# Reordering ScalarE's queue in the attentions of a two-block transformer kernel: a unit's high half ahead of the exponentials, the copy of turned probabilities ahead of the filling unit's evacuation

## The chip, the core and the metric

One core of a Trainium2 chip runs the whole program. The metric is device time in microseconds of one execution; the kernel before has a median of 2870.46 us over three runs.

## What is computed

Two blocks of two layers each, on one sequence of S = 256 tokens with D = 1024 channels, all in float32. A layer of the first block mixes tokens in three ways (8-head forgetting attention with a causal mask, a short convolution, a chunkwise gated recurrence), projects back, and then applies a SwiGLU (layer 0) or a routed mixture of eight experts (layer 1). A layer of the second block runs three attentions side by side, all with 8 heads:

```python
y_a = _gqa_axial(q, k, v, ...)          # softmax(q k) v, rotary by row and column
y_b = _diff_attention(q, k, v, lam, ..) # (softmax(q1 k1) - lam * softmax(q2 k2)) v
y_c = _mla(c_q, c_kv, k_r, ...)         # latent attention
merged = jnp.sum(gates * jnp.einsum('bsne,ned->bsnd', y, w_branch[l]), axis=2)
x = x + merged @ w_out[l]
x = x + jnp.square(jax.nn.relu(h2 @ w_ff1[l])) @ w_ff2[l]
```

## The kernel before

**Weights come as units.** All weight matrices are cut into 550 units of 128 x 2048 float32 (1 MB). Each engine has its own program, and all take the units in the same order. SP loads unit s into `raw[s % 4]` (L451) once VectorE has finished with the unit four before it. TensorE's fast path takes numbers in two parts, so ScalarE copies the unit to its high half, `whi[s % 3]` (`split_hi`, L500), after the load has landed and after TensorE has used unit s - 3, and VectorE then subtracts it from the unit to get the low half, `wlo[s % 3]` (`split_lo`, L843). TensorE multiplies in three products (high by high, high by low, low by high, `mm3`), all recorded at L1373. ScalarE and VectorE split two units ahead of the one that TensorE works on: `take()` on each of them moves the stream on by one unit and splits unit s + 2 (LEAD = 2). Except for the loads' queue, nothing is scheduled at run time: the order of each engine is that of its program, and semaphores tie them together.

**Projections.** `out_of(bank, dst, ...)` on ScalarE (L524) is: `take()`, wait until TensorE has used the unit, then evacuate the PSUM bank into its place in SBUF (L527).

**Attentions.** An attention is a list of jobs, each of four heads and 128 queries. Before it, projections that are not yet needed are put into a list of *fillers* on every engine; the attention takes one of them in every iteration, or in every second one (`fill_every=2`), so that TensorE has something to do while ScalarE and VectorE work on a softmax. A filler's product always goes to PSUM bank 7, and TensorE starts the next filler only when bank 7 has been evacuated. The loop has two iterations more than there are jobs. In iteration n:

- TensorE (`attention`, L1472): scores of job n into banks 0 and 1 or 2 and 3; then, for job n - 2, the weighing of the values with the turned probabilities `pt`, into bank 6 (it waits for the copy of `pt`); then the filler, 48 matmuls of 256 columns into bank 7; then the transposes of job n - 1's probabilities (L1519, `ident`) into banks 4 and 5, once VectorE has normalized them.
- VectorE (L917): in the first mixer, bias and mask (L932) and row maximum (L936), else the row maximum straight from PSUM (L938); then, if there is a filler, the low half of a unit (L843), and behind the first mixer's first filler also the short convolution (L976 to L983), which waits for that filler's evacuation; then it waits for the exponentials, takes the reciprocal of the sums (L944), and normalizes (L946). In the difference attention every second job is combined with the one before it (L950), and only these jobs are transposed and weighed.
- ScalarE (L549): four exponentials (L563, each with its sum), after the maximum; the evacuation of bank 6 for job n - 2 (`y` or `yT`, L568); then the filler (`fill`, L529, in iterations that have one): the high half of the unit two ahead (L500) and the evacuation of bank 7 (L527); then the copy of the transposed probabilities of job n - 1 from banks 4 and 5 to `pt` (L579), once TensorE has turned them.

There are eight attentions in the program: in each of two layers of the first block one `fox_heads` attention of 4 jobs (6 iterations, 2 fillers: `cc1`, and `rgs` with the function Silu); in each of two layers of the second block an axial one of 4 jobs (6 iterations, 6 fillers), a difference one of 8 jobs (10 iterations, `fill_every=2`, 5 fillers: Tanh into `sg`), and a latent one of 4 jobs without fillers. ScalarE's functions come from tables; a change from Exp to Silu or back puts a table load ahead of the instruction, while the copies run under any table, and Exp and Tanh without a load between them.

The order inside ScalarE's iteration is what the change touches:

Of the kernel before, what the change touches and what calls it, by code (L numbers as in the profile page):

```python
# [114 lines left out]
def build(nc, io):  # L115
    ctx = ExitStack()
    with ctx:
        def sem(name):
            return ctx.enter_context(nc.semaphore(name))
# [4 lines left out]
        hi_ready, lo_ready, unit_used = sem("hi_ready"), sem("lo_ready"), sem("unit_used")  # L124
# [3 lines left out]
        drained = sem("projection_drained")  # L128
# [95 lines left out]
        PS = ctx.enter_context(nc.psum_tensor("PS", [P, 8, 512], F32))  # L224

        def banks(b, n):
            return PS[:, b:b + n, :].rearrange("p b c -> p (b c)")
# [255 lines left out]
        def scalar_program(act):  # L483
            C = Counts()
            stream = Count()
            fillers = []

            def after(sem, k=1):
                act.wait_ge(sem, C.next(sem, k))
# [6 lines left out]
            def split_hi(s):  # L496
                act.wait_ge(raw_landed[s % RAW], 16 * (s // RAW + 1))
                if s >= SPLIT:
                    act.wait_ge(unit_used, s - SPLIT + 1)
                act.activation(whi[s % SPLIT][:], raw[s % RAW][:], ACT.Copy).then_inc(hi_ready, 1)  # L500

            def take():

                s = stream.next() - 1
                if s + LEAD < U_ALL:
                    split_hi(s + LEAD)
                return s + 1
# [16 lines left out]
            def out_of(bank, dst, scale=1.0, func=ACT.Copy, wide=None):  # L524
                act.wait_ge(unit_used, take())
                src = PS[:, bank, :] if wide is None else PS[:, bank, :].rearrange("p (t c) -> p t c", t=wide)
                act.activation(dst, src, func, scale=scale).then_inc(drained, 1)  # L527
                C.next(drained)

            def fill(n=1):  # L530
                for _ in range(min(n, len(fillers))):
                    f = fillers.pop(0)
                    out_of(7, f.dst, f.scale, f.func, f.wide)

            def head_square(src, sq):
                act.activation(sq, src, ACT.Square).then_inc(hn_squared, 1)

# [5 lines left out]
            def head_norm(src, nt, rows_, scale, sq):  # L543
                head_square(src, sq)
                fill()
                head_root(SUMS, rows_, scale)
                fill()

            def attention(jobs, pbs, pts, fill_every=1):  # L549
                turned_before, mixed_before = C.now(turned), C.now(mixed)  # L550
                turns = list(itertools.accumulate(j.value is not None for j in jobs))
                k = 0
                for n in range(len(jobs) + 2):
                    if n < len(jobs):
                        j, pb, b, w = jobs[n], pbs[n % PB], 2 * (n % 2), jobs[n].keys
                        sp = PS[:, b:b + 2, :].rearrange("p b (h k) -> p b h k", h=2)
                        m, z = stat[:, n % PB, 0:4], stat[:, n % PB, 4:8]
                        if n >= PB:
                            act.wait_ge(turned, turned_before + turns[n - PB + (jobs[n - PB].value is None)])
                        after(max_ready)  # L560
                        for i in range(4):
                            src = pb[:, i, 0:w] if j.bias else sp[:, i // 2, i % 2, 0:w]
                            ins = act.activation(pb[:, i, 0:w], src, ACT.Exp, bias=m[:, i:i + 1],  # L563
                                                 accum_out=z[:, i:i + 1])
                        ins.then_inc(exped, 1)
                    if n >= 2 and jobs[n - 2].value:
                        after(mixed)
                        act.activation(jobs[n - 2].dst, PS[:, 6, 0:2 * P].rearrange("p (t q) -> p t q", t=2),  # L568
                                       ACT.Copy).then_inc(mixed_out, 1)
                        C.next(mixed_out)  # L570
                    if n % fill_every == 0:
                        fill()
                    if 1 <= n <= len(jobs) and jobs[n - 1].value:
                        kb = jobs[n - 1].keys // P
                        tp = banks(4, 2).rearrange("p (h b q) -> p h b q", h=4, b=NT)
                        after(turned)
                        if k >= 2:
                            act.wait_ge(mixed, mixed_before + k - 1)
                        act.activation(pts[k % 2][:, :, 0:kb, :], tp[:, :, 0:kb, :], ACT.Copy).then_inc(pt_ready, 1)  # L579
                        k += 1  # L580

            def first_mixer(l):
                out_of(6, flat(zf))
# [26 lines left out]
                out_of(6, pair(qkT, 3))  # L610
                act.wait_ge(drained, C.now(drained))
                head_square(qkT[:], hT[:])
                cum_exp()
                out_of(7, vtok[:, :, 0:UC], wide=NT)
# [9 lines left out]

                fillers.extend(waiting_projections1(l))
                attention(fox_heads(l), pb1, pt1)
                fill(len(fillers))

# [88 lines left out]
            def second_mixer(l):  # L717
# [11 lines left out]
                after(va_turned)  # L729
                act.activation(va[:].rearrange("p t c -> p (t c)"), PS[:, 4, 0:S], ACT.Copy).then_inc(va_ready, 1)  # L730
                attention(axial_heads(), pb2, pt2)

                fill(max(0, len(fillers) - 15))
                fill()
                fill()
                C.next(rope_done)
                attention(diff_heads(), pb2, pt2, fill_every=2)
                act.wait_ge(mixed_out, C.now(mixed_out))
                head_norm(y2[:, 4:8, :], 4, 16, 1.0 / HD, hT[:, 0:4, :])
# [1227 lines left out]
        with nc.Block() as block:  # L1967
            block.sync(sync_program)
            block.scalar(scalar_program)
            block.vector(vector_program)  # L1970
            block.tensor(tensor_program)
# [160 lines left out]
```

## Time and profile before

| | |
|---|---|
| runs | 2867.01, 2870.46, 2870.82 us |
| profiled execution | 2872.48 us, its span 2870.7 us |
| TensorE matmul busy | 2617.0 us, 91% |
| VectorE busy | 1857.6 us, 65% |
| ScalarE busy | 1496.9 us, 52% |
| TensorE's granted clock, mean | 0.948 |
| copies to `pt`, L579 | 32, 31.2 us |
| exponentials, L563 | 160 |
| high halves, L500 | 550 of 1.91 us, 1051.9 us |
| low halves, L843 | 550 of 2.29 us, 1259.5 us |

The times of matmuls overlap: one of 256 columns is recorded with about 0.28 us, and the next starts about 0.12 us behind it. "Idle before" of a row is the time for which its engine did nothing, with the instruction that ended the wait. The clock is told as a share of 2.4 GHz, and has two levels, 1.0 and 0.5. A row of the timeline with x4 or x16 stands for so many instructions, its duration from the first's start to the last's end.

### The profile page before, as it was taken

Reading aid. Unit: us, or ns where it says so; the run is one execution under the profiler, and the core shown is the slowest. Engines: PE = TensorE matmul, PEld = TensorE weight load, DVE = VectorE, ACT = ScalarE, POOL = GpSimd, SP = SyncE. Lnnn points to the kernel's source line nnn. Section 1 sums busy time; section 2 is a strip of 40 time slices with the busy share of each in tenths; the row PEclk is TensorE's granted clock in tenths of the full one; section 3 lists DMA queues with packets and bytes.
Section 4 is the critical chain, followed back from the end, with each engine's and each line's share of the span. In section 5 each row is a group of like instructions: output and inputs, shape, how many; then the busy total and the mean of one; then the engine's idle time right before and its main releaser. Section 6 shows DMA issues by size and latency. Waiting matters only on the chain.

```text
span 2870.7 us, 38623 instructions
## 1 busy us (share of the span) xinstructions
PE 2617.0 (91%) x16826; PEld 2329.6 (81%) x16826; DVE 1857.6 (65%) x1580; ACT 1496.9 (52%) x1442; POOL 0.2 (0%) x4
## 2 busy tenths in 40 slices
PE   6879999887899999999999997988799989878998
PEld 6769998766787878878787786877689988768998
DVE  4645445564688888888888885555565554546554
ACT  4244334433577777777776774445444444544443
POOL 0000000000000000000000000000000000000000
PEclk9879999997999999999999998999899999889999
DMA  5214554221499989989999894323145543223452
GB/s 203 89 59 146 178 190 149 101 89 59 177 366 349 368 348 360 355 347 367 348 364 351 352 358 169 133 89 133 44 162 180 189 145 118 83 94 116 149 191 89
DMA packets 83100, 585.32 MB, mean 204 GB/s; under 512 B 9481, under 2 KB 11209, under 8 KB 12273
## 3 DMA queue, kind: packets, MB, share of 16 engines
q1 hardware_dynamic: 82928, 582.81, 54.4%
q8 instruction: 135, 2.21, 0.3%
q14 instruction: 37, 0.30, 0.0%
HBM read 581.73 MB, written 1.05 MB: 203 GB/s over the span
## 4 chain that ended last, share of the span: by engine, by line
PE 82%; DVE 10%; ACT 6%; issue 1%; DMA 0%; ACTq 0%; SPq 0%; DVEq 0%
PE PS L1373 80%; ACT whi L500 2%; DVE wlo L843 2%; ACT pb L563 2%; PE PS L1757 1%; PE PS L1519 1%; ACT pt L579 1%; DVE hT L860 1%; DVE stat L938 1%; DVE pb L946 1%; DVE small L856 1%; DVE hT L911 0%; DVE pb L932 0%; DVE qe L1004 0%; DVE ke L1003 0%
## 5 line engine op out<-in xcount | busy, mean ns | idle before, releaser
L843 DVE TENSOR_TENSOR wlo<-raw,whi 128x2048 fp32r<-128x2048 f32 x550 | 1259.5, 2291 | 568.3 <-ACT whi L500 558.3
L500 ACT ACTIVATE whi<-raw 128x2048 fp32r<-128x2048 f32 x550 | 1051.9, 1913 | 375.5 <-PE PS L1373 374.6
L1373 PE MATMUL PS<-hhi,whi 128*128 128x256 f32 x1952 | 572.3, 293 | 31.9 <-DVE hlo L866 19.0
L1373 PE MATMUL PS<-hlo,whi 128*128 128x256 f32 x1952 | 563.3, 289 | 0.0
L1373 PE MATMUL PS<-hhi,wlo 128*128 128x256 f32 x1952 | 562.5, 288 | 0.0
L1373 PEld LDWEIGHTS PS<-hhi,whi 128*128 128x128 f32 x1952 | 384.9, 197 | 46.7 <-issue 40.4
L1373 PEld LDWEIGHTS PS<-hlo,whi 128*128 128x128 f32 x1952 | 385.9, 198 | 0.6 <-issue 0.5
L1373 PEld LDWEIGHTS PS<-hhi,wlo 128*128 128x128 f32 x1952 | 385.1, 197 | 0.0
L1373 PE MATMUL PS<-whi,xghi 128*128 128x512 f32 x896 | 360.1, 402 | 2.1 <-ACT pm L667 2.1
L1373 PE MATMUL PS<-whi,xglo 128*128 128x512 f32 x896 | 355.2, 396 | 0.0
L1373 PE MATMUL PS<-wlo,xghi 128*128 128x512 f32 x896 | 355.0, 396 | 0.0
L1373 PEld LDWEIGHTS PS<-whi,xglo 128*128 128x128 f32 x896 | 169.2, 189 | 40.7
L1373 PEld LDWEIGHTS PS<-whi,xghi 128*128 128x128 f32 x896 | 169.2, 189 | 40.6 <-issue 2.1
L1373 PEld LDWEIGHTS PS<-wlo,xghi 128*128 128x128 f32 x896 | 169.3, 189 | 37.5
L1373 PE MATMUL PS<-whi,mahi 128*128 128x512 f32 x448 | 177.9, 397 | 1.9 <-DVE malo L1191 1.9
L1373 PE MATMUL PS<-whi,malo 128*128 128x512 f32 x448 | 178.0, 397 | 0.0
L1373 PE MATMUL PS<-wlo,mahi 128*128 128x512 f32 x448 | 177.9, 397 | 0.0
L1373 PE MATMUL PS<-bhi,wlo 128*128 128x256 f32 x512 | 144.1, 281 | 0.0
L1373 PE MATMUL PS<-bhi,whi 128*128 128x256 f32 x512 | 143.7, 281 | 0.0
L1373 PE MATMUL PS<-blo,whi 128*128 128x256 f32 x512 | 142.6, 279 | 0.0
L563 ACT ACTIVATE pb<-PS,stat 128x256 f32<-128x256 f32 x128 | 58.9, 472 | 116.6 <-DVE stat L938 109.3
L1373 PEld LDWEIGHTS PS<-whi,mahi 128*128 128x128 f32 x448 | 84.8, 189 | 22.1 <-DVE wlo L843 2.1
(331 smaller groups left out, 3720.2 us busy)
## 6 DMA issues: line engine op xcount, KB each, us to landing
raw<-in_wm SPq DMA_DIRECT2D x336, 1024.0 KB, 4.9
raw<-in_ws SPq DMA_DIRECT2D x214, 1024.0 KB, 4.8
xT<-in_xT SPq DMA_DIRECT2D x1, 1024.0 KB, 4.8
bsum<-in_bsum SPq DMA_DIRECT2D x1, 1024.0 KB
out_T<-hT SPq DMA_DIRECT2D x4, 256.0 KB, 2.5
lmask<-in_lmask SPq DMA_DIRECT2D x1, 512.0 KB
tri<-in_tri SPq DMA_DIRECT2D x1, 256.0 KB
cmask<-in_cmask SPq DMA_DIRECT2D x1, 256.0 KB
```

Source lines behind the costliest of these rows:

```text
L500: act.activation(whi[s % SPLIT][:], raw[s % RAW][:], ACT.Copy).then_inc(hi_ready, 1)
L563: ins = act.activation(pb[:, i, 0:w], src, ACT.Exp, bias=m[:, i:i + 1], accum_out=z[:, i:i + 1])
L579: act.activation(pts[k % 2][:, :, 0:kb, :], tp[:, :, 0:kb, :], ACT.Copy).then_inc(pt_ready, 1)
L843: dve.tensor_tensor(wlo[s % SPLIT][:], raw[s % RAW][:], whi[s % SPLIT][:].bitcast(F32), ALU.subtract).then_inc(lo_ready, 1)
L856: step(dve.reciprocal(rstd, rstd))
L860: ins = dve.scalar_tensor_tensor(out=hT[:, t, :], in0=xT[:, t, :], scalar=gain(t), in1=rstd, op0=ALU.mult, op1=ALU.mult)
L938: dve.tensor_reduce(m.rearrange("p (b h) -> p b h", b=2), sp[:, :, :, 0:w], AX, ALU.max, negate=True).then_inc(max_ready, 1)
L946: ins = dve.tensor_scalar(pb[:, i, 0:w], pb[:, i, 0:w], z[:, i:i + 1], None, ALU.mult)
L1373: return pe.matmul(out, a, b, start=start, stop=stop, skip_group_check=True)
L1519: ins = pe.transpose(tp[:, i, b, :], buf[:, i, b * P:(b + 1) * P], ident[:])
L1757: ins = pe.transpose(PS[:, 6, f * P:(f + 1) * P], mact[:, f * P:(f + 1) * P], ident[:])
```

## The change

In an iteration with a filler, ScalarE now takes the filler at the start of the iteration: `split_ahead` makes the high half of the unit two ahead before it waits for the maximum. The evacuation of bank 7 is left for the end of the iteration: `take_out` runs behind the copy to `pt`. VectorE's, TensorE's and SP's programs are unchanged, and so are the iterations without a filler.

```diff
+            def split_ahead():
+
+                return (fillers.pop(0), take()) if fillers else None
+
+            def take_out(filled):
+                if filled:
+                    f, used = filled
+                    act.wait_ge(unit_used, used)
+                    src = PS[:, 7, :] if f.wide is None else PS[:, 7, :].rearrange("p (t c) -> p t c", t=f.wide)
+                    act.activation(f.dst, src, f.func, scale=f.scale).then_inc(drained, 1)
+                    C.next(drained)
...
                 for n in range(len(jobs) + 2):
+                    filled = split_ahead() if n % fill_every == 0 else None
                     if n < len(jobs):
...
                                        ACT.Copy).then_inc(mixed_out, 1)
                         C.next(mixed_out)
-                    if n % fill_every == 0:
-                        fill()
                     if 1 <= n <= len(jobs) and jobs[n - 1].value:
...
                         k += 1
+                    take_out(filled)
```

## Rows read from the trace of the kernel before

**Rows 1.** The page, part 4: the chain that ended last, by engine.
```profile
PE 82%; DVE 10%; ACT 6%; issue 1%; DMA 0%; ACTq 0%; SPq 0%; DVEq 0%
```

**Rows 2.** Waits, 1886 to 1975 us and 145 to 192 us: us in total, times, longest.
```profile
PE PS L1373 <- ACT pt L579: 11.0, 4, 4.2
...
PE PS L1373 <- ACT pt L579: 9.8, 4, 4.5
```

**Rows 3.** Timeline of ScalarE, first mixer, layer 0: start, us, engine, line, op.
```profile
154.52 0.60 ACT L527 ACTIVATE cc<-PS 128x512 f32<-128x512 f32 x1 [0.59 <-PE PS L1373]
...
163.24 0.40 ACT L563 ACTIVATE pb<-pb,stat 128x128 f32<-128x128 f32 x1 [8.13 <-DVE stat L936]
...
164.80 1.89 ACT L500 ACTIVATE whi<-raw 128x2048 fp32r<-128x2048 f32 x1
166.71 1.28 ACT L527 ACT_TABLE_LOAD   x1
168.01 0.60 ACT L527 ACTIVATE rgs<-PS 128x512 f32<-128x512 f32 x1
168.50 0.59 ACT L579 ACTIVATE pt<-PS 128x512 f32<-128x512 f32 x1
```

**Rows 4.** Timeline of VectorE, first mixer, layer 0.
```profile
156.18 0.68 DVE L977 TENSOR_TENSOR cu<-cc,cx 128x512 f32<-128x512 f32 x1
...
159.76 0.69 DVE L983 TENSOR_TENSOR yT<-cb,cy 128x512 f32<-128x512 f32 x1
...
171.62 1.22 DVE L936 TENSOR_REDUCE stat<-pb 128x4 f32<-128x1024 f32 x1
```

**Rows 5.** Timeline of TensorE, first mixer, layer 0: the weighing of job 0.
```profile
169.24 1.12 PE L1373 MATMUL PS<-pt,vtok 128*64 128x128 f32 x8 [4.48 <-ACT pt L579]
```

**Rows 6.** Timeline of ScalarE, difference attention, layer 0, iteration 2.
```profile
1906.59 0.47 ACT L563 ACTIVATE pb<-PS,stat 128x256 f32<-128x256 f32 x1 [3.88 <-DVE stat L938]
...
1908.40 1.92 ACT L500 ACTIVATE whi<-raw 128x2048 fp32r<-128x2048 f32 x1
...
1910.67 1.04 ACT L579 ACTIVATE pt<-PS 128x1024 f32<-128x1024 f32 x1
```

**Rows 7.** Timeline of VectorE, difference attention, layer 0: three maxima and a low half.
```profile
1905.34 1.22 DVE L938 TENSOR_REDUCE stat<-PS 128x4 f32<-128x1024 f32 x1
1910.35 2.29 DVE L843 TENSOR_TENSOR wlo<-raw,whi 128x2048 fp32r<-128x2048 f32 x1 [3.79 <-ACT whi L500]
...
1913.94 1.23 DVE L938 TENSOR_REDUCE stat<-PS 128x4 f32<-128x1024 f32 x1
...
1919.76 1.22 DVE L938 TENSOR_REDUCE stat<-PS 128x4 f32<-128x1024 f32 x1
```

**Rows 8.** Timeline of TensorE, difference attention, layer 0: weighings, transposes, scores.
```profile
1911.86 1.97 PE L1373 MATMUL PS<-pt,vb 128*64 128x128 f32 x16 [4.17 <-ACT pt L579]
...
1926.34 1.09 PE L1373 MATMUL PS<-pt,vb 128*64 128x128 f32 x16 [1.40 <-ACT pt L579]
...
1934.52 1.06 PE L1519 MATMUL PS<-ident,pb 128*128 128x128 f32 x8
1935.52 1.13 PE L1373 MATMUL PS<-qkb 32*128 32x256 f32 x8
1940.88 1.97 PE L1373 MATMUL PS<-pt,vb 128*64 128x128 f32 x16 [4.23 <-ACT pt L579]
1950.00 1.04 PE L1519 MATMUL PS<-ident,pb 128*128 128x128 f32 x8
```

**Rows 9.** Windows: us, busy of PE, PEld, DVE, ACT, POOL, then PEclk, DMA, GB/s.
```profile
1911.80:1918.60 6.80, 6.74 (x37) 5.61 (x38) 4.66 (x13) 2.20 (x9) 0.00 (x0) 0.50 0.48 157
...
1925.00:1935.00 10.00, 8.57 (x77) 7.87 (x78) 7.80 (x14) 3.40 (x11) 0.00 (x0) 1.00 0.30 107
```

**Rows 10.** Timeline, axial attention, layer 0: the copy, and the next filler's first matmul.
```profile
1835.83 1.03 ACT L579 ACTIVATE pt<-PS 128x1024 f32<-128x1024 f32 x1 [0.28 <-PE PS L1519]
...
1838.03 0.39 PE L1373 MATMUL PS<-hhi,whi 128*128 128x256 f32 x1
```

## The prediction

> **What bounds the kernel now.** I read the chain that ended last first: TensorE has 82% of it, so only what makes TensorE wait is worth anything, however long ScalarE or VectorE sit idle [rows 1]. Then the table of waits, once over the first mixer's attention of layer 0 (145 to 192 us) and once over the difference attention of layer 0 (1886 to 1975 us): in both TensorE's longest waits are for the copy `pt` at L579, 9.8 us in 4 waits and 11.0 us in 4 waits, the longest 4.5 and 4.2 us [rows 2]. The layer 1 stretches have the same pattern, and so count twice. Last the timelines, to see what stands ahead of that copy.
>
> First mixer: job 0's transposes are done before the second exponentials even start (163.24), but the copy starts at 168.50, because ScalarE still has, in this order, exponentials, a high half (1.89), a table load (1.28) and the evacuation of `rgs` (0.60) ahead of it [rows 3]. TensorE stands 4.48 us for the copy, from the end of its scores at 164.76 to 169.24 [rows 5].
>
> Difference attention: exponentials end at 1908.40, then high half (1.92) and evacuation come, and the copy runs at 1910.67 [rows 6]. TensorE waits 4.17, 1.40 and 4.23 us for it in three successive pairs of jobs [rows 8]. VectorE suffers too: its low half waits for the high half, and its reciprocal and normalization stand behind the low half in its own queue [rows 7].
>
> **Part by part.** Nothing is added or removed: the same instructions run, in another order, on ScalarE only, and only in iterations that have a filler. VectorE's and TensorE's programs are untouched, and SP's loads wait only for low halves, which come no later. One wait moves forward, that of the high half for its buffer: it needs the unit before the filler's to be used, which TensorE has done before the scores that the exponentials need anyway. I cost it at nothing.
>
> *First mixer, iterations 0 and 1.* At iteration 0 the high half runs where ScalarE idled, in front of the Exp table load, so the first exponentials come some 0.2 us later. VectorE covers that: the convolution can start only when the filler is evacuated, at 155.12 [rows 3], and takes 4.3 us to 160.45 today; it now starts at 155.15 in place of 156.2, 1.0 us sooner [rows 4]. So normalization and the next maximum, for which the exponentials waited until 163.24 [rows 3], are done at 162.2. In iteration 1 the high half (155.1 to 157.0) is long over by then. Exponentials take 1.6 us as today (163.24 to 164.80) and run 162.2 to 163.9, the copy of 0.59 ends at 164.5, and TensorE begins to weigh as soon as its scores end, 164.8, in place of 169.24: **4.4 us**. The other side keeps pace: the low half starts right behind the maximum, 162.2 to 164.5, with its high half long ready, and the third maximum moves from 171.62 + 1.22 = 172.84 to 168.4 [rows 4], also 4.4 earlier. The two table loads and the evacuation now stand behind the copy, 164.4 to 167.6, ahead of exponentials that cannot start before 168.4: covered with 0.8 us to spare. From there VectorE's and ScalarE's chain runs as before, so 4.4 us per layer stay, 8.8 in all.
>
> *A rule against it.* The row shows a table load of 1.28 us with the next instruction 0.02 us behind it [rows 3]. The Trainium skill (ScalarE: Activation LUTs, What ACT_TABLE_LOAD costs) adds a drain of about 1.38 us to each switch. By it the two loads would reach 170.3, 1.9 us past the maximum, and the two first mixers would give 5.0 us in place of 8.8. I go by the row.
>
> *Difference attentions, even iterations.* Take the time from one weighing to the next.
> First weighing: the high half now runs in the 3.88 us that ScalarE idles before its exponentials [rows 6], so the copy follows them at 1908.40 instead of 1910.67: **2.3 us**.
> Then a period of two jobs, today 1926.34 - 1911.86 = 14.48 and 1940.88 - 1926.34 = 14.54 us [rows 8]. It becomes the longer of two loops. TensorE: weighing, scores and filler from 1926.34 to the transposes at 1934.52 are 8.18 us at full clock [rows 9], transposes 1.06, and 1.2 from their end through the copy (1.04) to the next weighing: 10.4 us. VectorE with ScalarE: from maximum to maximum 8.60 us in the filler's job (1905.34 to 1913.94) and 5.82 in the other (to 1919.76) [rows 7]; in the first, the low half (2.29) ended at 1912.64, with the reciprocal right behind it; it now starts right behind the maximum and ends at 1905.34 + 1.22 + 2.29 = 1908.85, 3.8 us sooner, and the loop is 4.8 + 5.8 = 10.6. So 10.6 us a period, **3.9 us** saved in each of two.
> Last stretch, weighing to transposes: 1950.00 - 1940.88 = 9.12 us today, part of it at the lower clock; the 8.18 above less one set of scores (1.1 [rows 8]) is 7.1: **2.0 us**.
> Sum 12.1 us per layer if TensorE keeps its clock. After the 4.17 us stall it ran 6.8 us at half its clock (1.2 GHz) [rows 9]. The stall left in that place is 1.9 us, which lies between the stall of 1.40, after which the row shows the full clock, and the longer ones; so the low clock costs nothing or some 1.7 us more there, of which half is slack against VectorE's loop. I take **11.6**, 23.2 for both, with 10.4 to 13 each.
>
> *Axial attentions.* A filler every iteration hides everything: the copy starts right behind the transposes already and the exponentials' chain has a whole iteration to spare. What changes is that the evacuation (0.60) follows the copy, which ends at 1836.86, so bank 7 is free at 1837.46, and the next filler starts there at 1838.03 [rows 10]: covered, with 0.57 us over. Nothing either way. The latent attentions have no filler and don't change.
>
> **Sum:** 8.8 + 23.2 = 32.0 us. The profiled execution took 2872.48 us (span 2870.7), 2.0 above the median of 2870.46; the difference holds for either, and from the median it gives 2838.5.
>
> **Rivals.**
> 1. *Only the copy's new place pays (0.10).* If VectorE and ScalarE slow each other when the low half runs beside the exponentials, the 3.8 us in VectorE's loop shrink. The timelines of these stretches never show the two side by side, so the bounds are a loss of nothing and of all 3.8. With all lost the period stays at 14.4 us and a difference attention gains 2.3 at the first weighing and 2.0 at the end, 4.3; with 4.4 for the first mixer, 2 x 8.7 = 17.4, hence 2853. For it: VectorE's loop is the longer of the two, so any slowing counts. Against: the exponentials read PSUM and the low half reads SBUF.
> 2. *Table switches cost more than their rows (0.07).* As above, 2.5 us per first mixer: 2842.5. Against it, instructions start 0.02 us behind each load.
> 3. *No change (0.04).* TensorE's stalls would have to reappear behind another releaser, or the clock stay low in both mixers. 2868.
> 4. *Slower: bank 7 (0.04).* The evacuation now stands behind a copy, the copy behind transposes, these behind VectorE's probabilities. If the copy's 1.03 and the evacuation's 0.60 were not under other work, the next filler would wait 1.6 us in each of 4 axial iterations per layer, 13 us in all, and in the difference attentions' iterations 2 to 8 too, another 13, in place of their gain; with the first mixers' 8.8 kept, 2870.5 + 26 - 8.8 = 2888. It decides where transposes' end to next filler falls below 1.66 us; today it is 2.2.
>
> **Numbers.** Forecast 0.75, 2838.5. Its own uncertainty is 2832 to 2844: clock (3 us), handoffs, and the first mixers. The range goes up to rival 1, and down for a clock better than assumed: 2831 to 2853. A difference under 0.2% (5.7 us) can't be told from none here. Faster 0.92, same 0.04, slower 0.04.
>
> **What would show it.** In the profile after: the wait for `pt` gone from the first mixer's 4.48 us place, and the copy ahead of the table load; waits of 4.17, 1.40 and 4.23 turned into about 1.9, 0.4 and 0.4; the low half right behind the maximum; weighings 10.6 us apart; the axial stretch as long as before, no wait for an evacuation ahead of a filler. Wrong would be: periods still near 14 us, exponentials or low halves longer than 0.47 and 2.29, a wait for `sg`, `vb` or `cc` on TensorE, or gaps that close but with the lower clock spread wider.

## The result, and the profile after

The kernel after takes 2833.36 us (median of four runs, 2829.06 to 2834.53), the kernel before 2868.74 in the same comparison. The ratio is 0.9871, with a 95% interval of 0.9858 to 0.9885: 37 us faster by the ratio (33 to 41), 35.4 by the medians. The forecast was 2838.5, in a range of 2831 to 2853.

The profiled execution took 2834.53 us, with a span of 2832.7 where the one before had 2870.7. The page after, parts 1 and 4: as many instructions, TensorE's busy time down by 20 us (its mean granted clock was 0.957 where it had been 0.948), and within a point the same shares on the chain [rows 1].

```profile
PE 2596.7 (92%) x16826; PEld 2309.6 (82%) x16826; DVE 1856.3 (66%) x1580; ACT 1494.7 (53%) x1442; POOL 0.2 (0%) x4
...
PE 82%; DVE 11%; ACT 5%; issue 1%; DMA 0%; ACTq 0%; SPq 0%; DVEq 0%
```

**Where the 38 us of span went.** Runs of one program differ by some 3 us in places that have nothing to do with the attentions (in the profiled ones, already ahead of the first mixer's attention). So I compare stretches, each from the start of an attention's first exponential to the start of the squares that ScalarE takes behind the attention (in latent attentions: the first `y2hi`). They hold one kind of attention each; the axial one and the difference one share a stretch, with the fillers and the rotation between them. (Split at the difference attention's first exponential, the axial part takes 69.77 and 69.72 us before and 69.82 and 69.63 after: all of the gain lies in the difference part.) Times in us, worked out from the starts in the timelines of ScalarE:

| stretch | before | after | difference |
|---|---|---|---|
| first mixer, layer 0 | 39.68 | 34.00 | -5.68 |
| first mixer, layer 1 | 39.68 | 34.02 | -5.66 |
| axial + difference, layer 0 | 131.40 | 119.02 | -12.38 |
| axial + difference, layer 1 | 131.31 | 118.83 | -12.48 |
| latent, layers 0 and 1 | 23.37, 23.39 | 21.58, 21.59 | -3.6 in all |
| everything else | | | +1.8 in all |

The latent attentions' 3.6 us are no work saved: the stretch ahead of them became 2.3 us longer in the same two layers (58.09 to 59.26 and 58.06 to 59.17), while the granted clock rose from 0.84 and 0.85 to 0.97 in the latent stretches and fell from 0.85 to 0.84 ahead of them. That leaves 1.3 us net.

**First mixer.** Timeline of ScalarE in the kernel after, first mixer, layer 0, against [rows 3]:

```profile
160.84 0.40 ACT L576 ACTIVATE pb<-pb,stat 128x128 f32<-128x128 f32 x1 [5.30 <-DVE stat L948]
...
162.40 0.57 ACT L590 ACTIVATE pt<-PS 128x512 f32<-128x512 f32 x1
162.99 1.28 ACT L544 ACT_TABLE_LOAD   x1
164.28 0.60 ACT L544 ACTIVATE rgs<-PS 128x512 f32<-128x512 f32 x1
164.90 1.28 ACT L576 ACT_TABLE_LOAD   x1
...
166.86 0.51 ACT L576 ACTIVATE pb<-pb,stat 128x256 f32<-128x256 f32 x1 [0.68 <-DVE stat L948]
```

And of TensorE, against [rows 5]:

```profile
163.31 0.66 PE L1385 MATMUL PS<-pt,vtok 128*64 128x128 f32 x8
...
169.82 0.66 PE L1385 MATMUL PS<-pt,vtok 128*64 128x128 f32 x8 [2.85 <-ACT pt L590]
...
176.57 1.98 PE L1385 MATMUL PS<-pt,vtok 128*64 128x128 f32 x16 [4.28 <-ACT pt L590]
...
181.65 1.09 PE L1385 MATMUL PS<-pt,vtok 128*64 128x128 f32 x16 [1.21 <-ACT pt L590]
```

The copy follows the exponentials directly, and both table loads and the evacuation lie behind it. The second load ends 0.68 us before the next exponentials start. The weighing of job 0 has no wait in its row, where 4.48 us stood. But TensorE's waits for `pt` over this attention have hardly shrunk: 9.8 us in 4 waits before, 8.3 in 3 now, since the next two weighings wait 2.85 and 4.28 us where they waited 0.43 and 3.72. What moved is VectorE's chain: counted from the first exponential, the third maximum ends at 17.58 us (165.60 + 1.22 less 149.24), where it was 22.37.

**Difference attention.** Timeline of ScalarE in the kernel after, layer 0, iteration 2, against [rows 6]:

```profile
1891.88 1.93 ACT L500 ACTIVATE whi<-raw 128x2048 fp32r<-128x2048 f32 x1
1895.88 0.47 ACT L576 ACTIVATE pb<-PS,stat 128x256 f32<-128x256 f32 x1 [2.07 <-DVE stat L950]
...
1897.69 1.03 ACT L590 ACTIVATE pt<-PS 128x1024 f32<-128x1024 f32 x1
1898.59 0.62 ACT L544 ACTIVATE sg<-PS 128x512 f32<-128x512 f32 x1
```

Of VectorE, against [rows 7]:

```profile
1894.62 1.22 DVE L950 TENSOR_REDUCE stat<-PS 128x4 f32<-128x1024 f32 x1
1895.76 2.28 DVE L855 TENSOR_TENSOR wlo<-raw,whi 128x2048 fp32r<-128x2048 f32 x1
...
1899.34 1.23 DVE L950 TENSOR_REDUCE stat<-PS 128x4 f32<-128x1024 f32 x1
1902.56 0.18 DVE L956 RECIPROCAL stat<-stat 128x4 f32<-128x4 f32 x1 [2.00 <-ACT pb L576]
...
1905.15 1.22 DVE L950 TENSOR_REDUCE stat<-PS 128x4 f32<-128x1024 f32 x1
```

And of TensorE, against [rows 8]:

```profile
1898.86 1.09 PE L1385 MATMUL PS<-pt,vb 128*64 128x128 f32 x16 [1.88 <-ACT pt L590]
...
1906.81 1.04 PE L1531 MATMUL PS<-ident,pb 128*128 128x128 f32 x8
...
1909.45 1.09 PE L1385 MATMUL PS<-pt,vb 128*64 128x128 f32 x16 [0.55 <-ACT pt L590]
...
1920.04 1.09 PE L1385 MATMUL PS<-pt,vb 128*64 128x128 f32 x16 [0.54 <-ACT pt L590]
1926.91 1.04 PE L1531 MATMUL PS<-ident,pb 128*128 128x128 f32 x8
```

The low half has no wait in its row any more and starts as the maximum ends. From maximum to maximum it is 4.72 and 5.81 us, 10.53 in all (8.60 and 5.82 before), and the weighings lie 10.59 us apart where 14.48 and 14.54 were. VectorE is not busy all the time in this loop: in the second job of a pair it waits 2.00 us for ScalarE's exponentials, before and after the change. The chain that closes runs through both engines.

### The profile page after: what moved, and what is told of

The parts are those of the page before. It is cut to its first block, busy times and chain, and to the rows that moved or that the text cites. A ratio compares the mean times of both kernels' runs of the same rounds, so it can differ in the third digit from the quotient of the medians.

```text
span 2832.7 us, 38623 instructions
## 1 busy us (share of the span) xinstructions
PE 2596.7 (92%) x16826; PEld 2309.6 (82%) x16826; DVE 1856.3 (66%) x1580; ACT 1494.7 (53%) x1442; POOL 0.2 (0%) x4
## 4 chain that ended last, share of the span: by engine, by line
PE 82%; DVE 11%; ACT 5%; issue 1%; DMA 0%; ACTq 0%; SPq 0%; DVEq 0%
PE PS L1385 81%; DVE wlo L855 2%; ACT whi L500 1%; ACT pb L576 1%; PE PS L1769 1%; DVE stat L950 1%; DVE pb L958 1%; ACT pt L590 1%; DVE hT L872 1%; DVE small L868 1%; PE PS L1531 1%; DVE hT L923 0%; DVE pb L944 0%; DVE qe L1016 0%; DVE ke L1015 0%
## 5 line engine op out<-in xcount | busy, mean ns | idle before, releaser
L1385 PEld LDWEIGHTS PS<-whi,malo 128*128 128x128 f32 x448 | 84.6, 189 | 20.5
```

The costliest lines, as they stand in the source:

```text
L1385: return pe.matmul(out, a, b, start=start, stop=stop, skip_group_check=True)
```

## The experiments

All ratios are against the kernel before, timed in the same batch. "Stretch" is the axial and difference stretch of the table above, unless another is named.

### Parts of the change: high half, and copy

Only the high half moved; against the kernel after:

```diff
+                    take_out(filled)
                     if 1 <= n <= len(jobs) and jobs[n - 1].value:
...
-                    take_out(filled)
```

> Only the high half is moved ahead of the exponentials; the evacuation of bank 7 stays where it was, between the evacuation of bank 6 and the copy of pt. Theory A (what pays is VectorE's loop: the low half right behind the maximum): nearly the whole gain, 33 to 35 us of the 35 to 38 seen. In a difference attention the copy of pt stands 0.5 us behind the exponentials, so the first weighing comes 0.5 later than with the whole change, but the weighings stay 10.6 us apart, as TensorE's loop of 10.4 has room. In the first mixer the weighing of job 0 comes 1.9 us later (table load and evacuation ahead of the copy), about 166.4 in place of 164.5 on the time scale of before, but the chain of maxima keeps its 4.4 us. Theory B (the copy's place pays): under half of the gain, and weighings more than 12 us apart. Theory C (TensorE's clock pays, the stalls only trigger it): the gain depends on the stall in front of the first weighing, 2.4 us here against 1.9, and up to 3.4 us per difference attention come back with a stretch at half the clock.

Measured: 2841.38 us, ratio 0.990 (0.9884 to 0.9917), so 29 us faster (24 to 33), under the 33 to 35 expected. In its profile the stretches are 33.79 and 34.01 us in the first mixers and 119.49 and 120.63 in the second block, together 34 us shorter than in the profiled execution before, and 32 against first mixers of 38.5 us, which other executions of unchanged code show (see the runs by attention below). TensorE's weighings there, in layer 0 and then in layer 1:

```profile
1899.03 1.09 PE L1385 MATMUL PS<-pt,vb 128*64 128x128 f32 x16 [2.37 <-ACT pt L591]
1909.62 1.09 PE L1385 MATMUL PS<-pt,vb 128*64 128x128 f32 x16 [0.55 <-ACT pt L591]
...
2435.22 1.09 PE L1385 MATMUL PS<-pt,vb 128*64 128x128 f32 x16 [2.37 <-ACT pt L591]
2446.89 1.09 PE L1385 MATMUL PS<-pt,vb 128*64 128x128 f32 x16
```

In layer 0 the weighings stay 10.59 us apart, as theory A said, with the stall in front at 2.37 and not 1.88. In layer 1 the same stall was followed by a stretch of low clock, here the windows of the 6.8 us behind each first weighing (us, busy of the engines, then the granted clock):

```profile
1899.00:1905.80 6.80, 6.77 (x63) 6.25 (x64) 4.72 (x8) 4.01 (x10) 0.00 (x0) 1.00 0.38 149
2435.20:2442.00 6.80, 6.79 (x50) 6.03 (x51) 4.73 (x8) 4.00 (x10) 0.00 (x0) 0.75 0.36 147
```

There the period was 11.67. So a stall of 2.4 us can, but need not, cost another 1.1 us by the clock. That is as much of theory C as this run shows.

With the high half moved, the copy's place is worth something: 29 us became 37, 8 more by the medians (2841.38 and 2833.36, timed in different batches; the two intervals just meet). The profiled executions, 2837.85 and 2834.53 us, differ by 3.3: 2.3 in the axial and difference stretches, and 1.6 in the latent attention of layer 1, which is 23.18 here. That execution was the fastest of four of its kernel, 3.5 under its median, and no trace shows what the slower ones lost; so the copy's share is 3 us in what the traces show, and up to 8.

Only the copy moved; against the kernel after:

```diff
-                    filled = split_ahead() if n % fill_every == 0 else None
                     if n < len(jobs):
...
                         C.next(mixed_out)
+                    filled = split_ahead() if n % fill_every == 0 else None
                     if 1 <= n <= len(jobs) and jobs[n - 1].value:
```

> Only the copy of pt is moved ahead of the evacuation of bank 7; the high half stays behind the exponentials. Theory A: next to nothing, 1 us in all (between 0 and 3): in a difference attention the first weighing comes 0.4 us sooner, and VectorE's loop still has the high and the low half in it, so the weighings stay 14.4 us apart; in the first mixer TensorE's stall of 4.48 us shrinks to 2.6, but the third maximum stays where it is, so the end doesn't move. Theory B: 17 us or more. Theory C: a little more than A says if the shorter stalls let the clock stay up, up to 6 us per difference attention.

Measured: 2870.17 us, ratio 1.000 (0.9991 to 1.001). The stretch is 131.01 and 131.22 us, and the weighings in layer 0 stay 14.48 and 14.54 us apart. VectorE there, layer 0:

```profile
1902.49 1.22 DVE L950 TENSOR_REDUCE stat<-PS 128x4 f32<-128x1024 f32 x1
1907.50 2.29 DVE L855 TENSOR_TENSOR wlo<-raw,whi 128x2048 fp32r<-128x2048 f32 x1 [3.79 <-ACT whi L500]
...
1911.09 1.23 DVE L950 TENSOR_REDUCE stat<-PS 128x4 f32<-128x1024 f32 x1
```

And TensorE's first weighing in the first mixer, layer 0, of this kernel:

```profile
163.19 0.66 PE L1385 MATMUL PS<-pt,vtok 128*64 128x128 f32 x8 [2.56 <-ACT pt L590]
```

Maximum to maximum is 8.60 us, exactly as before. In the first mixer TensorE's 4.48 us stall shrank to 2.56, as expected, and bought nothing: the first mixers take 38.52 and 38.48 us, as with unchanged code (38.53 and 38.48 in the run with the change in the difference attentions alone). This settles the main question: the copy's place by itself is worth nothing within 3 us, and the high half's place by itself gives 29 of the 37 us, since VectorE's low half waits for it and VectorE's normalization waits behind the low half. The copy's place pays only on top of that.

### Parts of the change: which attention

A switch `ahead` picks, per attention, the new or the old order:

```diff
-                    filled = split_ahead() if n % fill_every == 0 else None
+                    filled = split_ahead() if ahead and n % fill_every == 0 else None
...
+                    if not ahead and n % fill_every == 0:
+                        fill()
...
-                attention(fox_heads(l), pb1, pt1)
+                attention(fox_heads(l), pb1, pt1, ahead=True)
```

> The whole change, but only in the two first mixers' attentions. From the two traces (first exponential to the squares behind the attention: 39.68 us before, 34.00 and 34.02 after) 11.3 us of gain; my forecast had 8.8. If parts add up, this and the run with the change in the difference attentions alone give the whole together, within 2 us. If the gain in the first mixer were lost again before the experts (which run at the rate of the loads), nothing or a few us would be left.

Measured: 2860.37 us, ratio 0.9966 (0.9954 to 0.9977), so 9.8 us faster (6.6 to 13.2), between the forecast's 8.8 and the 11.3 of the two traces. Its first mixers take 33.72 and 34.03 us, its second-block stretches 131.40 and 131.43, as before. The gain is still there behind the experts.

> The whole change, but only in the two difference attentions. From the two traces (first exponential of the axial attention to the squares behind the difference attention: 131.40 and 131.31 us before, 119.02 and 118.83 after) 24.9 us of gain, if the axial attention has no share in it, as I forecast (my forecast was 23.2 here). If the axial attention has a share, less by that share.

Measured: 2839.59 us, ratio 0.9898 (0.9882 to 0.9915), so 29 us faster (24 to 34). Its stretch is 118.98 and 119.06 us, the whole change's value. These two give 24.7 of the 29, and the latent attentions with the stretches ahead of them 1.2 net, as in the kernel after; the rest isn't traced. Its first mixers, with unchanged code, take 38.53 and 38.48 us, and so do those of the run with the copy alone (38.52, 38.48). The 39.68 of the profiled execution before is thus one of two lengths that the old code shows. They go with the clock from the third exponentials on, in layer 0: it was 0.50 there in the profile before (172.9 to 190.15 us), and 0.70 in this one (168.7 to 185.09). Of the 5.7 us by which the profiles differ, 4.5 are the change's, and 1.2 go with the clock, by luck.

> The whole change, but only in the two axial attentions. My forecast: nothing, within 1 us of the kernel before, and the stretch from the first exponential of the axial attention to the squares behind the difference attention at 131.3 us. The runs with the change in the other two kinds add up to 39 to 41 us by their medians against 35 to 37 for the whole; if the axial attentions cost the difference, this one is slower than before by 2 to 5 us.

Measured: 2869.69 us, ratio 0.9996 (0.9987 to 1.0006), and stretches of 131.52 and 131.45 us. Nothing, as forecast. The parts' gains (10 and 29 us) and the whole (37) agree within their intervals.

### What sets the period: VectorE's loop

One more VectorE pass behind the low half, in the jobs with a filler:

```diff
                     if n % fill_every == 0:
                         fill()
+                        for _ in range(more if n < len(jobs) else 0):
+                            step(dve.tensor_tensor(hT[:, 0:2, :], xT[:, 0:2, :], xT[:, 0:2, :], ALU.add))
```

> The kernel after, with one extra VectorE pass of 0.69 us (0.75 with its wait) behind the low half in each of the first four fillers' jobs of the difference attentions. If VectorE's loop is the longer one, as I had it (10.6 against 10.4), the weighings move from 10.59 to 11.3 us apart, and the stretch from the first exponential of the axial attention to the squares behind the difference attention grows by 2.1 us (119.0 to 121.1). If TensorE's loop were the bound, the first half of the pass would be hidden: periods under 11.0 and under 1 us.

Measured in a single execution, which was profiled (2845.92 us, so its time as a whole says little): TensorE's weighings in layer 0.

```profile
1900.07 1.09 PE L1387 MATMUL PS<-pt,vb 128*64 128x128 f32 x16 [1.89 <-ACT pt L590]
...
1911.39 1.09 PE L1387 MATMUL PS<-pt,vb 128*64 128x128 f32 x16 [1.28 <-ACT pt L590]
...
1922.71 1.09 PE L1387 MATMUL PS<-pt,vb 128*64 128x128 f32 x16 [1.27 <-ACT pt L590]
```

11.32 us apart, 0.73 more than 10.59: the pass is paid for in full, and TensorE's stall of 0.55 grows to 1.28 by the same 0.73. The stretch is 120.82 and 120.88 us (121.1 expected), 3.9 us more in all. The execution took 11.4 us longer than the profiled one of the kernel after: 3.7 of the rest lie in the latent attentions, whose clock is back at 0.84 and 0.79, and 3.6 ahead of the second block, where no code differs. The loop that runs through VectorE is the bound in the kernel after too.

### What the clock is worth

The kernel before, with extra matmuls of `ident` by `xT` where TensorE waits for the copy in the difference attentions:

```diff
+            def hold(bank, n):
+                for _ in range(n):
+                    mm(PS[:, bank, 0:S], ident[:], xT[:, 0, :], True, True)
...
                         claim(6)
+                        hold(6, doses.get(n, 0))
                         after(pt_ready)
...
-                attention(diff_heads(), pb2, pt2, fill_every=2)
+                attention(diff_heads(), pb2, pt2, fill_every=2, doses={3: 12, 5: 12, 7: 12, 9: 3})
```

> The kernel before, with 12, 12, 12 and 3 extra matmuls of 0.27 us (into bank 6, overwritten by the weighing) in the difference attentions, where TensorE waits for the copy of pt, so that its clock should stay up while it waits. Theory A (VectorE's loop sets the period): the weighings stay 14.4 us apart whatever the clock; only the last stretch, from the last weighing before the last filler to the transposes, shrinks from 9.1 to 7.2 us, so 2 us per difference attention and 4 in all. Theory C (the stalls cost mostly by the clock they pull down): the periods shrink too, 5 to 6 us per difference attention, 10 to 12 in all.

Measured: 2871.19 us, ratio 1.0007 (0.9997 to 1.0016), stretches 131.15 and 131.75. The dose was wrong: one of them takes 0.45 us and not the 0.27 I had taken from the scores' rate, so 12 outlasted the stall and made a period of 15.34. The run says little, and was repeated with 8, 8, 8 and 2.

> The kernel before, with extra matmuls as in the run with 12, but 8, 8, 8 and 2: one took 0.45 us and not 0.27 there, so that 12 of them outlasted the stall and TensorE set the period (15.34 us). 8 take 3.6 us and fit into it. Theory A (VectorE's loop sets the period): with the clock up, the weighings stay 14.4 us apart, and TensorE waits a little for the copy of pt behind the extra matmuls in every period; the stretch from the first exponential of the axial attention to the squares behind the difference attention falls by 2 to 3 us (131.4 to about 129), all of it behind the last of the three weighings. Theory C (the lower clock is what the stalls cost): it falls by 5 or more.

Measured: 2867.93 us, ratio 0.9993 (0.9984 to 1.0003). The stretch is 130.28 and 130.34 us, 1.0 to 1.1 below the kernel before. TensorE's weighings in layer 0, and the window over all of them with its granted clock:

```profile
1911.63 1.09 PE L1373 MATMUL PS<-pt,vb 128*64 128x128 f32 x16 [0.43 <-ACT pt L579]
...
1926.11 1.09 PE L1373 MATMUL PS<-pt,vb 128*64 128x128 f32 x16 [0.49 <-ACT pt L579]
...
1940.65 1.09 PE L1373 MATMUL PS<-pt,vb 128*64 128x128 f32 x16 [0.49 <-ACT pt L579]
1948.93 1.06 PE L1524 MATMUL PS<-ident,pb 128*128 128x128 f32 x8 [1.25 <-DVE pb L950]
```

```profile
1907.00:1950.00 43.00, 40.05 (x303) 34.54 (x300) 25.54 (x42) 23.74 (x61) 0.00 (x0) 1.00 0.21 74
```

The clock was at its upper level (2.4 GHz) throughout, and the periods are 14.48 and 14.54 us: to a hundredth those of the kernel before, where TensorE ran 6.8 us at the lower level after the first stall [rows 9]. A slower TensorE only used up the slack it had against VectorE. Only behind the last weighing is there something to gain, and there too VectorE's probabilities come next, after 1.25 us of waiting, so that 1 us remains of the 2 that I expected. Theory C falls for the periods.

### How much slack bank 7 has

The kernel after, with three extra copies on ScalarE ahead of each late evacuation in the axial attentions:

```diff
             def take_out(filled, late=0):
                 if filled:
+                    for _ in range(late):
+                        step(act.activation(hT[:, 0:2, :], xT[:, 0:2, :], ACT.Copy))
...
-                attention(axial_heads(), pb2, pt2)
+                attention(axial_heads(), pb2, pt2, late=3)
```

> The kernel after, with three extra copies on ScalarE of 0.62 us each, with a wait for each other, ahead of every late evacuation in the axial attentions: 1.9 to 2.1 us. My forecast had 0.57 us of slack between the evacuation of bank 7 and the next filler, so TensorE should now wait 1.3 to 1.5 us ahead of four fillers per layer (those of iterations 2 to 5), 5 to 6 us per layer and 10 to 12 in all over the kernel after. If there is no slack (rival 4), 7.5 to 8.5 per layer, 15 to 17 in all; if bank 7 is never waited for, nothing.

Measured: 2852.97 us, ratio 0.9939 (0.9925 to 0.9954), some 17 to 20 us above the kernel after. TensorE's waits over the axial attention of layer 0:

```profile
PE PS L1387 <- ACT cc L546: 4.1, 3, 1.4
PE PS L1387 <- ACT pt L592: 2.4, 2, 1.2
PE PS L1387 <- ACT vb L546: 1.4, 1, 1.4
PE PS L1387 <- ACT sg L546: 0.8, 1, 0.8
```

Four waits for bank 7 are new, 1.4 us each, as 2.0 us of delay less 0.6 of slack makes, and 5.5 in all (the fifth, for `sg`, and the two for `pt` are in the kernel after too, with the same lengths). But 10 to 12 us in all were expected. The stretch grew by 7.2 us in layer 0 (126.24) and by 8.1 in layer 1 (126.90), near the 7.5 to 8.5 that stood for no slack; so the totals alone would not tell the two apart, and the single waits do. Behind the third wait of layer 0 the clock was 0.82 (1848.1 to 1857.7 us), so a wait can cost more than its own length. The two latent attentions took 4.8 us more, at a lower clock; no run tells what lowered it there. Rival 4's mechanism is real, and each wait starts where the forecast had put it; the change stays 0.6 us on the right side of it.

### A faster version

The profile after shows what is left in the first mixers: a low clock where TensorE is on the chain. The kernel after with `hold` at such places, into the bank that TensorE fills next (bank 6 ahead of a weighing); the first dose repeated the mistake above:

```diff
-                attention(fox_heads(l), pb1, pt1)
+                attention(fox_heads(l), pb1, pt1, doses={3: 9, 4: 13, 5: 3})
...
-                head_norm(DK, lambda t: selw[:, t, :], lambda t: selT[:, t, :], 16, hT, [4, 5])
+                head_norm(DK, lambda t: selw[:, t, :], lambda t: selT[:, t, :], 16, hT, [4, 5], held=(7, 9))
...
+                claim(6)
+                hold(6, 22)
                 after(rope_done)
...
-                attention(latent_heads(), pb2, pt2)
+                attention(latent_heads(), pb2, pt2, doses={3: 2, 4: 7, 5: 3})
```

> The kernel after, with extra matmuls of 0.27 us where TensorE waits in the first mixers (9, 13 and 3 ahead of the weighings, 7 and 9 around the sums of squares) and in the latent attentions (22 behind the rotation, 2, 7 and 3 ahead of the weighings). Theory A says that the clock is a term of its own: where TensorE's own work is on the chain (weighing and transposes at the end of the first mixer, the 16 sums, scores behind the rotation) it costs 2 to 5 us per place, so 6 to 16 us in all below the kernel after. If what waits is bound by VectorE and ScalarE alone, within 3 us of the kernel after.

Measured: 2848.87 us, ratio 0.9915 (0.9898 to 0.9933), 15 us slower than the kernel after, where 6 to 16 us faster was expected. The doses outlasted the stalls: the first mixers took 39.26 and 37.09 us in place of 34.0. In layer 0 the first dose also started late, 2.3 us behind the matmul before it, as bank 6 came free only then. With doses of 0.45 us each and bank 7:

```diff
+                        if n in doses:
+                            claim(7)
+                            hold(7, doses[n])
                         claim(6)
...
-                attention(fox_heads(l), pb1, pt1)
+                attention(fox_heads(l), pb1, pt1, doses={3: 5, 4: 8, 5: 2})
...
-                head_norm(DK, lambda t: selw[:, t, :], lambda t: selT[:, t, :], 16, hT, [4, 5])
+                head_norm(DK, lambda t: selw[:, t, :], lambda t: selT[:, t, :], 16, hT, [4, 5], held=(5, 6))
...
+                claim(7)
+                hold(7, 13)
                 after(rope_done)
...
-                attention(latent_heads(), pb2, pt2)
+                attention(latent_heads(), pb2, pt2, doses={3: 1, 4: 4, 5: 2})
```

> The kernel after, with fewer extra matmuls than in the first run of this kind, where they outlasted the stalls (0.45 us each and not 0.27, and some could start only when bank 6 was evacuated): 5, 8 and 2 ahead of the weighings in the first mixers, 5 and 6 around the sums of squares, 13 behind the rotation and 1, 4 and 2 ahead of the weighings in the latent attentions, all into bank 7. From the stretches at half the clock in the kernel after: the first mixer's end has some 17 us of them, of which TensorE is on the chain for about 6 us per layer, so 3 us a layer; the latent attentions 13 us, with about 3 us on the chain. Expected: 6 to 12 us below the kernel after. If the doses still outlast the stalls somewhere, or what waits is bound by VectorE and ScalarE, between 3 us below and 5 above.

Measured: 2823.80 us, ratio 0.9841 (0.9825 to 0.9857): 46 us faster than before, and so some 9 us faster than the kernel after (timed in another batch; the two intervals just fail to meet), as expected. The windows from 169 to 194 us, first of the kernel after, then of this one:

```profile
169.00:194.00 25.00, 13.89 (x72) 8.15 (x72) 7.11 (x16) 9.37 (x18) 0.00 (x0) 0.66 0.00 1
```

```profile
169.00:194.00 25.00, 21.00 (x132) 15.05 (x130) 10.47 (x25) 10.72 (x21) 0.00 (x0) 1.00 0.00 1
```

The clock is 1.00 in place of 0.66. The first mixers fall to 32.24 and 32.26 us, and the stretches behind them (sums of squares, projection) from 39.11 and 39.19 to 36.36 and 35.92: about 4.8 us per layer. In the latent attentions nothing is gained (21.69 and 21.66), but the stretch ahead of them falls from 59.26 and 59.17 to 57.54 and 57.49. The parts add up to 13 us, against the 9 measured.

## Why the prediction was right, point by point

- **First mixer, 4.4 us a layer.** The old code takes 38.5 us when its clock is as in most runs, the new one 34.0: 4.5. Of these 0.15 are no gain, as the first exponentials, from which the stretch is counted, come that much later behind the maximum (0.2 forecast). The profiled execution before happened to be a longer one (39.68), which made it 5.7. The slack of 0.8 us that I gave the two table loads measured 0.68. The evacuation starts 0.01 us behind the end of its load here too; the drain that the Trainium skill (ScalarE: Activation LUTs, What ACT_TABLE_LOAD costs) adds to a switch has no row, and the 5.0 us that it left the two first mixers is less than the 9.8 (6.6 to 13.2) that the change in them alone gave. Rival 2 falls, for these loads. (Its time is 2842.3 by its own terms, not 2842.5.)
- **Difference attention, 12.1 us with its clock, 11.6 taken.** First weighing 2.3: from the first scores to the first weighing it was 22.14 us before (1889.72 to 1911.86) and 19.80 after (1879.06 to 1898.86), 2.3. The periods: 3.9 each, measured 3.89 and 3.95; 10.6 against 10.59. The last stretch 2.0: measured 9.12 - 6.87 = 2.25. Sum 12.4, 0.8 above the 11.6 that I took. Of these, 0.5 are the step about the clock, which was too cautious: I took off 0.5 us for a low clock behind the remaining stall of 1.9, and none was lost in either layer's profile. A stall of 2.4 did lose 1.1 in one layer of two. The other 0.3 is the last stretch: weighing to transposes took 7.95 us with a filler and a set of scores and 6.87 without the scores, where I had 8.18 and 7.1.
- **What sets the period.** I had VectorE's loop by a narrow margin, 10.6 against 10.4 for TensorE's. With 7.95 in place of 8.18, TensorE's is 10.2. The order held: an extra 0.73 us there was paid in full, and TensorE at full clock in the kernel before changed nothing.
- **Axial attentions, nothing.** Measured nothing, with 0.6 us of slack at bank 7 as read from [rows 10].
- **Rivals.** Rival 1 (VectorE and ScalarE slow each other) falls on the durations: with the low half beside the exponentials, the low half takes 2.28 us, and the median exponential 0.473, as before; a few exponentials reach 0.499 instead of 0.482. But its title, that only the copy's place pays, was the wrong way round: the copy's place alone gives nothing. Its 2.3 us at the first weighing need the high half out of the way as well, and so did the account I gave of that step, where I spoke of the copy following the exponentials without saying that of the 2.27 us between them 1.8 are the high half's. Rival 3, no change, lies outside the interval. Rival 4 asked for less than 1.66 us from the end of the transposes to the next filler; the change left 0.6 us of room. The forecast did not foresee that in the first mixer TensorE would wait for `pt` nearly as long as before, at the next two jobs. That cost nothing of the 4.4 us, since they were taken from the maxima and not from that wait.
- **The total.** 32.0 forecast, 37 measured by the ratio (33 to 41) and 35.4 by the medians. The time lies in the range, and the 32.0 just below the interval of the gain. The attentions' stretches give 9.0 (against 38.5) and 24.9, so 33.9. The other 1.5 to 3 us were in no term of the sum: 1.3 are the latent attentions and the stretches ahead of them, with the clock at 0.97 in place of 0.84, and the rest isn't traced. That they added to the gain is luck.

## What to carry to other kernels

Where an engine waits for another's result, don't stop at the instruction that ends its wait: follow each loop round all engines, add up what must follow what in it, and move what lies on the longest. Here TensorE stalled for ScalarE's copy, but moving that copy alone gave nothing; the longest loop closed through VectorE, which waited for a high half that ScalarE could have made in its idle time. In a queue that runs in program order, put work that others need and that has its inputs early (the high half) into the idle time ahead of a wait, and work that nobody needs soon (the evacuation) behind what someone stands for, and then measure how far behind it may go.

## What the runs showed of the hardware that I had not expected

- A lower clock of TensorE behind a stall costs only where TensorE is on the chain. In the difference attentions of the kernel before, holding it up by extra matmuls gave 1 us of a stretch of 131; in the first mixers' ends and the sums and projection behind them it gave 4.8 us a layer of 73.
- The same stall of 2.37 us was followed by low clock in one layer and by full clock in the other of the same execution. The one of 1.88 us was followed by full clock in both.
- One extra 128 x 128 by 256 float32 matmul took 0.45 us (8 of them 3.72), recorded as two instructions, against 0.13 us for each of the 8 instructions of a job's scores; 16 instructions of two jobs' scores, which take their 32 channels from different partitions, took 1.16 us where 8 of one job took 1.13. No run tells why.
- From the squares behind the first mixer of layer 1 to the second block's first exponential it took 1170.1 to 1171.2 us in nine profiled executions without extra matmuls there (those of the kernels before and after among them), but 1173.9 with the copy alone and 1174.8 with the extra VectorE pass, whose code there is the same. No run tells why.
